# Gates and unit rows in one stage per layer, and four norms ahead of the attentions in one stage

## What is computed

```
# each of the two layers, 8 heads of width 128
q = l2_norm(dq) * (DN_DK ** -0.5);  k = l2_norm(dk)
beta = sigmoid(dn_b);  g = -exp(a_log) * softplus(dn_a + dt_bias)    # g is summed along the tokens
# second block
y = y * silu(z)
yg = yg * rsqrt(mean(yg * yg) + EPS) * ssd_norm_w        # 4 groups of 256
dq, dk = partial_rope(rms_norm(dq or dk, w), positions)  # 12 heads of 64 each
mqn = rms_norm(mq, mem_q_norm_w)                         # 4 heads of 192
```

## Time and profile before

| | us |
|---|---|
| median of 3 runs | 3886.69 (3882.48 to 3887.02) |
| the profiled execution | 3885.37 |
| its span, first to last instruction | 3883.6 |
| mean granted clock of PE | 0.948 |
| `delta_gates` and `delta_unit`, per layer (2 layers) | 42.5 |
| `ssd_norm`, `dilated_norm`, `rope`, `memory_q_norm` | 74.0 |

### The profile page before, as it was taken

How to read it: one execution, slowest core, us unless ns; L and a number is a source line. 1 busy time by engine, 2 the same in 40 slices (tenths; PEclk the granted TensorE clock), 3 DMA queues, 4 the chain that set the end, 5 groups by cost and what they waited for, 6 DMA issues and landing times. The chain is left out here.

```text
span 3883.6 us, 55109 instructions
## 1 busy us (share of the span) xinstructions
PE 3519.4 (91%) x21873; PEld 3100.0 (80%) x21873; DVE 2527.0 (65%) x3060; ACT 1897.1 (49%) x2038; POOL 56.0 (1%) x36
## 2 busy tenths in 40 slices
PE   4998889989797799999999996798588999999999
PEld 4978779989687487777877776797377999977887
DVE  6747456478455388888888873453564688495665
ACT  2534434354333376766767652353253444464554
POOL 0000000000000000000000000000000000000000
PEclk9999889989898799999999997899799899999999
DMA  6730336458011299999999972353022455503554
GB/s 222 252 133 6 109 142 237 164 192 307 5 66 44 109 357 359 363 360 364 365 361 362 360 272 98 112 193 109 7 87 98 162 184 180 183 17 126 193 194 157
DMA packets 296870, 739.08 MB, mean 190 GB/s; under 512 B 17449, under 2 KB 17904, under 8 KB 291312
## 3 DMA queue, kind: packets, MB, share of 16 engines
q1 hardware_dynamic: 296688, 736.60, 53.6%
HBM read 735.50 MB, written 1.05 MB: 190 GB/s over the span
## 5 line engine op out<-in xcount | busy, mean ns | idle before, releaser
L2064 DVE TENSOR_TENSOR weight_ring_low<-weight_ring,weights_high 128x2048 fp32r<-128x2048 f32 x336 | 773.7, 2345 | 149.7 <-ACT weights_high L2010 149.7
L2010 ACT ACTIVATE weights_high<-weight_ring 128x2048 fp32r<-128x2048 f32 x336 | 618.6, 1907 | 7.9 <-DMA weight_ring<-in_moe_w 7.7
L378 PE MATMUL psum_all<-h_high_projections,high_projections 128*128 128x256 f32 x1536 | 439.6, 286 | 25.4 <-DVE h_low_projections L313 25.4
L378 PE MATMUL psum_all<-h_low_projections,high_projections 128*128 128x256 f32 x1536 | 435.7, 284 | 0.0
L378 PE MATMUL psum_all<-h_high_projections,weight_ring_low 128*128 128x256 f32 x1536 | 431.6, 281 | 0.0
L1952 PE MATMUL psum_all<-weights_high,expert_in_turn_high 128*128 128x512 f32 x896 | 359.6, 401 | 18.0 <-DVE weight_ring_low L2064 11.8
L1952 PE MATMUL psum_all<-weights_high,expert_in_turn_low 128*128 128x512 f32 x896 | 356.9, 398 | 0.0
L1952 PE MATMUL psum_all<-weight_ring_low,expert_in_turn_high 128*128 128x512 f32 x896 | 352.1, 393 | 0.0
L378 PEld LDWEIGHTS psum_all<-h_high_projections,high_projections 128*128 128x128 f32 x1536 | 291.6, 190 | 29.8 <-DVE h_low_projections L313 29.7
L2952 PE MATMUL psum_all<-peer_h_high,expert_rows_high 128*128 128x256 f32 x1024 | 291.0, 284 | 5.0 <-DVE expert_rows_low L3000 5.0
L378 PEld LDWEIGHTS psum_all<-h_high_projections,weight_ring_low 128*128 128x128 f32 x1536 | 295.5, 192 | 0.0
(11 more groups left out here) (619 smaller groups left out, 7962.9 us busy)
## 6 DMA issues: line engine op xcount, KB each, us to landing
weight_ring<-in_moe_w SPq DMA_DIRECT2D x336, 1024.0 KB, 5.1
weight_ring<-in_w_in SPq DMA_DIRECT2D x48, 2048.0 KB, 8.6
expert_rows<-in_peer_down SPq DMA_DIRECT2D x128, 512.0 KB, 3.2
expert_rows<-in_peer_up SPq DMA_DIRECT2D x128, 512.0 KB, 3.2
weight_ring<-in_ffn_halves SPq DMA_DIRECT2D x42, 1024.0 KB, 6.3
branch_out<-in_ada_w SPq DMA_DIRECT2D x64, 512.0 KB, 9.8
weight_ring<-in_w_out SPq DMA_DIRECT2D x6, 2048.0 KB, 8.3
weight_ring<-in_ada_w SPq DMA_DIRECT2D x4, 2048.0 KB, 11.6
```

The lines of the kernel that those rows point to most:

```text
L378: mm = pe.matmul(half(k.ps, 4 * (g % R) + j), w[:, c, j * P:(j + 1) * P], x[:, c], start=(c == 0 and n == 0), stop=(c == KC - 1 and n == 2))
L2010: act.activation(high[:, q, h * HALF:(h + 1) * HALF], k.ring[:, q, h * HALF:(h + 1) * HALF], ACT.Copy).then_inc(high_made[q], 1)
L2064: dve.tensor_tensor(k.low[:, q, part], k.ring[:, q, part], high[:, q, part].bitcast(F32), ALU.subtract).then_inc(low_made[q], 1)
```

## The change

- `head_gates` and `unit_rows` go. `delta_heads` does both for one layer in one stage `delta_heads`. PE's order in it: gate projections, sums of squares, turns, broadcasts of the gates, broadcasts of the unit rows into all eight banks. ACT's order: squares, the chain of the gates, sigmoid, root, the four copies.
- `ssd_gates` is a function of its own, with the same work less one memset and one wait.
- `memory_unit` is left for `memory_k_norm` alone and loses the two small operations of ACT.
- The Silu of the gate goes to the end of ACT's queue in `ssd_heads`.
- `ssd_norm`, `dilated_norm`, `rope` and `memory_q_norm` become one stage, `second_norms`. The sums of the three norms fall on partitions 0, 32 and 64 of three banks, so that one tile `rs` holds them, with one root and one reciprocal over 68 partitions. The broadcasts read all 128 partitions of `rs`.

The new functions, cut (unchanged and minor lines left out):

```diff
+def delta_heads(k, l, gcol, grow, bcol, brow):
+    n, ia, w, rows = DNH, 2 * l, k.wba[:, l], 16
+    x = k.proj[:, Q0:Q0 + 16]
...
+        with k.stage(f"delta_heads{l}") as st:
...
+            @block.gpsimd
+            def _(pool):
...
+            @block.tensor
+            def _(pe):
+                for m, first in enumerate((n, 0)):
+                    for c in range(KC):
+                        mm = pe.matmul(k.ps[0:n, m, 0:T], w[:, c, first:first + n], k.h[:, c], start=(c == 0), stop=(c == KC - 1))
+                    mm.then_inc(projected, 1)
+                for b in range(16):
+                    pe.wait_ge(squared, b // 2 + 1)
+                    mm = pe.matmul(k.ps[0:rows, 3, 0:T], k.pick[:, 15 - b:15 - b + rows], sq[:, b], start=(b == 0), stop=(b == 15))
+                mm.then_inc(summed, 1)
+                pe.wait_ge(has_beta, 1)
+                pe.wait_ge(sums, 1)
+                for m, tile in enumerate((g, beta)):
...
+                        mm = pe.transpose(k.ps[:, 2, (2 * m + i) * n:(2 * m + i + 1) * n], tile[0:n, i * P:(i + 1) * P], k.ident[0:n, 0:n])
+                mm.then_inc(turned, 1)
                 done = 0
+                for tile in (g, beta):
                     for hh in range(0, n, 4):
                         if done >= 2:
                             pe.wait_ge(moved, done - 1)
...
                         mm.then_inc(spread, 1)
                         done += 1
+                pe.wait_ge(turned_out, 2)
+                pe.wait_ge(inverse, 1)
+                for i in range(8):
+                    if i >= 4:
+                        pe.wait_ge(moved, 3 + (i - 4) // 2)
+                    for e in range(2):
...
+                        mm = pe.matmul(k.ps[:, i, e * T:e * T + T], k.ident[:, b:b + 1].to_broadcast([P, P]), rs[:], start=True, stop=True)
+                    mm.then_inc(unit_spread, 1)
             @block.vector
             def _(dve):
...
                 dve.wait_ge(projected, 1)
+                dve.tensor_scalar(z[:], k.ps[0:n, 0, 0:T], k.hp[0:n, ia + 1:ia + 2], None, ALU.add).then_inc(biased, 1)
                 dve.wait_ge(logged, 1)
...
+                dve.wait_ge(summed, 1)
+                dve.tensor_scalar(rs[0:rows], k.ps[0:rows, 3, 0:T], k.qk_scale[0:rows], k.qk_eps[0:rows], ALU.mult, ALU.add).then_inc(mean, 1)
                 dve.wait_ge(turned, 1)
+                for m, cols in enumerate((gcol, bcol)):
                     dve.tensor_copy(cols[:], k.ps[:, 2, 2 * m * n:(2 * m + 2) * n].rearrange("p (i h) -> p i h", i=TT)).then_inc(turned_out, 1)
+                dve.wait_ge(root, 1)
+                dve.reciprocal(rs[0:rows], rs[0:rows]).then_inc(inverse, 1)
+                for i in range(8):
+                    dve.wait_ge(unit_spread, i + 1)
...
+                    dve.tensor_tensor(y, y, k.ps[:, i, :].rearrange("p (c t) -> p c t", c=2), ALU.mult).then_inc(unit, 1)
             @block.scalar
             def _(act):
+                for i in range(8):
+                    act.activation(sq[:, 2 * i:2 * i + 2], x[:, 2 * i:2 * i + 2], ACT.Square).then_inc(squared, 1)
                 act.wait_ge(biased, 1)
...
+                act.activation(sp_[:], sp_[:], ACT.Ln, bias=1.0).then_inc(logged, 1)
+                act.wait_ge(projected, 2)
...
+                act.activation(beta[0:n], k.ps[0:n, 1, 0:T], ACT.Sigmoid).then_inc(has_beta, 1)
+                act.wait_ge(mean, 1)
+                act.activation(rs[0:rows], rs[0:rows], ACT.Sqrt).then_inc(root, 1)
                 done = 0
+                for out in (grow, brow):
                     for hh in range(0, n, 4):
                         act.wait_ge(spread, done + 1)
+                        act.activation(out[:, hh:hh + 4], place_rows(k.ps, P)[:, 8 + 4 * (done % 2):12 + 4 * (done % 2)], ACT.Copy).then_inc(moved, 1)
                         done += 1
```

```diff
+def second_norms(k, masks, parts):
+    DIL, SSD, MEM = 0, 32, 64
+    z = k.proj[:, ZZ0:ZZ0 + 8]
+    o = k.o[:, 0:8]
+    x = k.proj[:, DQ0:DQ0 + 12]
+    q = k.proj[:, MQ0:MQ0 + 6]
+    sq_dil = k.proj[:, XS0:XS0 + 12]
+    sq_ssd = k.h
...
+        with k.stage("second_norms") as st:
...
             @block.gpsimd
             def _(pool):
...
+                pool.memset(rs[:], 1.0).then_inc(cleared, 1)
+                pool.tensor_copy(pairs_dil[:], col_bc(k.ident[:, DIL:DIL + 24], 64)).then_inc(paired, 1)
+                pool.tensor_copy(pairs_mem[:], col_bc(k.ident[:, MEM:MEM + MH], 64)).then_inc(paired, 1)
             @block.sync
             def _(sp):
...
                 sp.dma_start(masks, k.a["table_dil"]).then_inc(in_masks, 16)
                 sp.wait_ge(in_masks, 16)
+            @block.scalar
+            def _(act):
+                for i in range(6):
+                    act.activation(sq_dil[:, 2 * i:2 * i + 2], x[:, 2 * i:2 * i + 2], ACT.Square).then_inc(dil_squared, 1)
+                for i in range(4):
+                    act.wait_ge(gated, i // 2 + 1)
+                    act.activation(sq_ssd[:, 2 * i:2 * i + 2], o[:, 2 * i:2 * i + 2], ACT.Square).then_inc(ssd_squared, 1)
+                for i in range(3):
+                    act.activation(sq_mem[:, 2 * i:2 * i + 2], q[:, 2 * i:2 * i + 2], ACT.Square).then_inc(mem_squared, 1)
+                for e in range(2):
+                    act.activation(wm[:, e:e + 1], k.col("mem_q", 1, 1), ACT.Copy, scale=half_mask(k, e)).then_inc(halved, 1)
+                act.wait_ge(mean, 3)
+                act.activation(rs[0:MEM + MH], rs[0:MEM + MH], ACT.Sqrt).then_inc(root, 1)
+                act.wait_ge(angled, 1)
+                act.activation(sn[:], sn[:], ACT.Sin).then_inc(sined, 1)
+                act.activation(cs[:], cs[:], ACT.Sin).then_inc(sined, 1)
             @block.tensor
             def _(pe):
                 pe.wait_ge(pos_f, 1)
+                pe.matmul(k.ps[:, 7, 0:T], k.ones[0:1, :], posf[:], start=True, stop=True).then_inc(positions, 1)
+                for b in range(12):
+                    pe.wait_ge(dil_squared, b // 2 + 1)
+                    mm = pe.matmul(k.ps[DIL:DIL + 24, 0, 0:T], k.pick64[:, 22 - 2 * b:46 - 2 * b], sq_dil[:, b], start=(b == 0), stop=(b == 11))
+                mm.then_inc(dil_summed, 1)
+                for b in range(8):
+                    pe.wait_ge(ssd_squared, b // 2 + 1)
+                    mm = pe.matmul(k.ps[SSD:SSD + SSG, 1, 0:T], k.pick[:, 15 - b // 2:15 - b // 2 + SSG], sq_ssd[:, b], start=(b == 0), stop=(b == 7))
+                mm.then_inc(ssd_summed, 1)
+                for b in range(6):
+                    pe.wait_ge(mem_squared, b // 2 + 1)
...
+                    mm = pe.matmul(k.ps[MEM:MEM + MH, 2, 0:T], select, sq_mem[:, b], start=(b == 0), stop=(b == 5))
+                mm.then_inc(mem_summed, 1)
...
+                def rotate(i):
+                    pe.wait_ge(unit, i + 1)
+                    pe.matmul(k.ps[:, 1 + i, :], k.perm, x[:, 2 * i:2 * i + 2], start=True, stop=True).then_inc(rotated, 1)
+                pe.wait_ge(paired, 2)
+                pe.wait_ge(inverse, 1)
+                for i in range(6):
+                    for e in range(2):
...
+                        mm = pe.matmul(k.ps[:, 1 + i, e * T:e * T + T], pairs_dil[:, 2 * b:2 * b + 2].rearrange("p h n -> p (h n)"), rs[:],
+                                       start=True, stop=True)
+                    mm.then_inc(dil_spread, 1)
+                for b in range(4):
+                    spread_mem(b, half(k.ps, (14, 15, 0, 1)[b])).then_inc(mem_spread, 1)
+                for i in range(6):
+                    rotate(i)
+                pe.wait_ge(turned, 1)
+                for b in range(4, 6):
+                    spread_mem(b, half(k.ps, 2 + b - 4)).then_inc(mem_spread, 1)
+                for g in range(SSG):
+                    pe.matmul(half(k.ps, 4 + g), k.ident[:, SSD + g:SSD + g + 1].to_broadcast([P, P]), rs[:], start=True, stop=True).then_inc(ssd_spread, 1)
             @block.vector
             def _(dve):
...
+                for i in range(2):
+                    dve.tensor_tensor(o[:, 4 * i:4 * i + 4], o[:, 4 * i:4 * i + 4], z[:, 4 * i:4 * i + 4], ALU.mult).then_inc(gated, 1)
                 dve.wait_ge(in_pos, 16)
                 dve.tensor_copy(posf[:], posi[:]).then_inc(pos_f, 1)
+                dve.wait_ge(positions, 1)
...
+                dve.wait_ge(cleared, 1)
+                for r0, n, bank, summed, count in ((DIL, 24, 0, dil_summed, 64), (SSD, SSG, 1, ssd_summed, 2 * P), (MEM, MH, 2, mem_summed, MD)):
+                    dve.wait_ge(summed, 1)
+                    dve.tensor_scalar(rs[r0:r0 + n], k.ps[r0:r0 + n, bank, 0:T], 1.0 / count, EPS, ALU.mult, ALU.add).then_inc(mean, 1)
...
                 dve.tensor_scalar(cs[:], cs[:], PI_MAX, -PI_MAX, ALU.min, ALU.max).then_inc(angled, 1)
+                dve.wait_ge(root, 1)
+                dve.reciprocal(rs[0:MEM + MH], rs[0:MEM + MH]).then_inc(inverse, 1)
+                for i in range(6):
```

(46 more changed lines are left out.)

246 lines of the change are left out of this document (79 added, 167 removed).

## The result

The changed kernel took 3828.5 us (median of 4 runs, 3826.3 to 3830.4) where the kernel before took 3886.9 beside it: a ratio of 0.9855, with a 95% interval of 0.984 to 0.987, or 58.4 us less (50.5 to 62). The forecast was 51.4 us less, 3835.3 us with a range from 3828 to 3846.

What follows compares the result with a forecast made beforehand. No engine fills these stages, so each lasts as long as its longest chain. 25.6 (`delta_heads`) + 25.4 (`second_norms`) + 0.4 (`memory_k_norm`) = 51.4 us less, giving 3835.3 us, range 3828 to 3846.

Steps and rivals of the forecast that it cites:

- Part 1: `delta_heads`, twice: the stage becomes PE alone, 29.8 us against 42.5; 12.8 us less a layer, 25.6 for both.
- my lower bound: In `delta_heads`: PE passes keep 0.2135 us, half the row's 0.427 at half clock, giving 13.3 us less a layer.
- Part 2: Tail of `ssd_heads`: two Silu end ACT's queue; stage 1.27 us longer, the next without 2.4 us of waiting for them.
- Part 3, steps 1 to 3: Start of `second_norms`: DVE's gate products and cast, PE's sums, then DVE's mean, sine and cosine operations and reciprocal, to 2749.4.
- step 2: `second_norms`, PE's first 54 passes: 11.7 us, plus 1.7 for a 3.4 us half-clock spell, so 13.4.
- Part 3, step 4: `second_norms`, PE's 24 and 8 spread passes and 6 rotation passes: 9.7 us, plus 1.7 for a half-clock spell, to 2760.8.
- Part 3, steps 5 and 6: End of `second_norms`: DVE's rope, memory and `ssd_norm` operations, 15.2 us, then the engines' meeting, 0.3; attentions begin at 2776.3.
- Part 4: Small things: `memory_k_norm` loses two ACT operations, 0.4 us; `ssd_gates`, the masks' and weight transfers give 0.
- work behind these stages must keep its length: Sign for stages behind the changed ones: attentions or `delta_inverse` longer by more than 3 us means the clock moved there.
- more half-clock spells: Rival, chance 0.15: a 6.4 us spell in each `delta_heads`, both in `second_norms` as long; price 9.4 us, giving 3844.7.
- Fewer spells: Rival, chance 0.12: no spells in `second_norms`, passes of 0.2135 us in `delta_heads`; 3.4 + 1.0 us, giving 3830.9.
- the small products can't hold the clock: Rival, chance 0.02: PE stays at half clock through the merged stages, price 74 us, giving 3909.

Runs made afterwards that it cites:

- the repeat: The changed kernel unaltered, run again for a second trace and more times: 3827.4 us, ratio 0.9855 to the kernel before.
- the repeat of the kernel before: The kernel before, unaltered, run again for its second trace: 3881.5 us, ratio 0.9993.
- the padded kernel: The changed kernel with eighteen chained DVE products at the end of each `delta_heads`, making it as long as the two old stages: 3863.1 us, ratio 0.9949.

## Why the prediction was right, and where it was off

The forecast of faster held. 3828.5 us is at the low end of the range (3828), and that it lies inside is in part luck: the repeat measured 3827.4, half a microsecond outside. The sum was 7 us short (3.6 by all executions). That the changed stages gave 50.9 us against 51.4 is in part luck too: part 1 gave 0.7 more than its term and part 3 1.2 less. By its own steps:

- *Part 1*, 29.8 us a stage forecast, 29.37 measured, and 13.2 a layer against 12.8. PE had no gap, root and reciprocal lay under the gate broadcasts. The layer 0 of the repeat, 31.04 us, had the half-clock spell that was named as a sign of being wrong, at 1.7 us. A pass took 0.2156 us (blocks of 32 follow each other 6.90 us apart), about midway between the 0.218 that I took and my lower bound.
- *Part 2*: ACT's tail and the meeting took 3.61 us behind the last exp, 3.58 forecast.
- *Part 3, steps 1 to 3*: PE's first pass 2.63 us after the start (2.75), and 17.44 us from there to the first spread (17.5). Two errors cancelled in step 2. The spell was 6.8 us, not 3.4, which costs 1.7 more; and passes of neighbouring sums overlapped where one chain ended and the next began, which saved about as much. I had not thought of that overlap.
- *Part 3, step 4* is the term of this part that was mis-sized: 11.4 us to the first rope operation forecast (9.7 and half a spell of 3.4), 12.8 measured, because the second spell was 6.8 us as well. It is why the part gave 24.2 and not 25.4.
- *Part 3, steps 5 and 6*: DVE's tail 15.15 us (15.2), the meeting 0.3 (0.3). The wait that the change adds, five operations ahead of the reciprocal, was priced at 1.3 us on the path. Taking it away moved the stage by 2.5, as the spell behind the gap was shorter (the spreads took 7.11 us instead of 8.40), and the kernel by nothing.
- *Part 4*: 0.4 forecast, 0.37 measured (0.65 against the repeat of the kernel before).
- *The step that failed* is the sentence that "work behind these stages must keep its length", which priced all stages behind at nothing. In the first pair of profiles they gave 8.2 us, against the repeat of the kernel before 4.8, in the medians some 4 to 7. No single stage that was named as a sign moved by 3 us (the attentions got 1.1 longer); the difference was spread over many. That this goes with the moment at which they begin is shown by the padded kernel, and that a single stage's share is TensorE's clock is shown by the equal work in the pairs of windows and by the broadcasts of `delta_norm`. That all of the 4 to 7 us are such shares is argued, not shown: they are a net of some twenty entries of 0.2 to 3 us with both signs, and a single execution carries as much (the projections ahead of the SSD took 221.0 us in one profile of the kernel before, 222.9 in the other and 224.0 in both of the kernel after).
- *Rivals*: more half-clock spells was half right, in `second_norms` both spells were as long as it said, but `delta_heads` had none in the profile after and one of 1.7 us in the repeat. Fewer spells did not happen, though the 3830.9 us of that rival is nearer to the measured time than my 3835.3: the time alone does not tell the mechanism. That the small products can't hold the clock did not happen: `delta_heads` stands at 1.00 (0.95 in the repeat).

What stays open: what fixes the moment at which the clock falls in `delta_norm`. Filling its gap put it off in one kernel and stopped it in none, and no run varied the arrival in small steps. Open too is why layer 1 repeats and layer 0 does not.

## What to carry to other kernels

Give TensorE other work of the same stage to do while a small chain of mean, root and reciprocal runs on other engines: this was worth 13 us in each layer (11.5 where a spell fell into it), and adding up single rows foretold it to 0.4 us. Put small products that don't depend on each other into different partition groups and interleave them: `second_norms` got 3.4 us shorter. Expect stages behind a changed one to move by 1 to 2 us each, once by 3, in either direction, when their arrival shifts against the clock; a gain of that size is believed only once repeated runs of the whole kernel show it.

## What the runs showed that I had not expected

- Products with 24, 4 and 4 rows of output in PSUM partitions 0, 32 and 64 run at the same time when they are issued in turn: 52 passes in 8.0 us instead of 12.3.
- Filling a gap of 2.7 us in `delta_norm` did not keep TensorE at full clock (broadcasts 5.36 us in one kernel; in the other the fall came 3.4 us later in the stage), filling one of 4.0 us in `second_norms` did (5.45 for 24 passes instead of 8.40).
- An unchanged stage with the same work on every engine, layer 1's `delta_norm`, took 19.2 or 17.0 to 17.1 us in eleven profiles, according to whether the stages between projection and mixer had taken 42.5 or 29.4 us. The same stage in layer 0 did not sort so.
